# Three decoder mixers on one core: weight splits moved, transposes regrouped, buffers of matmul operands at other places

## What is computed

```
proj = rmsnorm(x) @ w_in                     # 512 x (512 + 512 + 64 + 2048)
c_q, c_kv, k_rope, gate = split(proj)
q  = rmsnorm(c_q) @ w_uq                     # per head 128 (nope) + 64 (rope)
kv = rmsnorm(c_kv) @ w_ukv                   # per head 128 (k) + 128 (v)
s  = (q_nope . k_nope + rope(q_rope) . rope(k_rope)) * scale, causal
y  = softmax(s) @ v
x  = x + (y * silu(gate)) @ w_out
```

## Time and profile before

| | |
|---|---|
| median of 3 runs | 2184.48 us (2184.06 to 2184.57) |
| the profiled execution | 2184.52 us |
| its span, first to last instruction | 2182.7 us |
| busy: PE, DVE, ACT, POOL | 99%, 66%, 45%, 6% of the span |
| matmuls | 10142 |
| DRAM traffic | 107 GB/s over the span |

### The profile page before, as it was taken

The page is one execution under the profiler, slowest core; times in us unless marked ns, Lnnn a source line. Parts: engine busy times, 40 slices in busy tenths (PEclk is TensorE's granted clock), DMA queues, the critical chain, the costliest instruction groups (busy, mean ns, idle before and its releaser), DMA issues. The chain is left out here.

```text
span 2182.7 us, 31173 instructions
## 1 busy us (share of the span) xinstructions
PE 2155.4 (99%) x10142; PEld 1791.6 (82%) x10142; DVE 1450.5 (66%) x2648; ACT 978.8 (45%) x1910; POOL 137.1 (6%) x161
## 2 busy tenths in 40 slices
PE   8999999999999999999999999999999999998999
PEld 6878888888888888888888888888888888887787
DVE  6677777777832568888888833676767676767432
ACT  5444444444432435555555633445453545355221
POOL 0100000000211000000000122200000000002000
PEclk9999999999999999999999999999999999999999
DMA  7312222222734623333333553532333233324542
GB/s 222 95 54 82 82 82 82 82 82 74 241 85 113 186 78 86 86 87 87 86 86 84 185 146 88 176 95 78 108 89 108 77 108 89 105 80 149 186 132 67
DMA packets 371436, 235.03 MB, mean 108 GB/s; under 512 B 5056, under 2 KB 345280, under 8 KB 371392
## 3 DMA queue, kind: packets, MB, share of 16 engines
q1 hardware_dynamic: 369264, 230.27, 36.8%
q10 hardware_dynamic: 2128, 4.19, 0.5%
HBM read 210.33 MB, written 24.12 MB: 107 GB/s over the span
## 5 line engine op out<-in xcount | busy, mean ns | idle before, releaser
L595 PE MATMUL pp<-act_hi,w_hi 128*128 128x512 f32 x2304 | 911.6, 396 | 11.7 <-DVE w_lo L569 9.2
L597 PE MATMUL pp<-act_hi,w_lo 128*128 128x512 f32 x2304 | 901.4, 391 | 0.0
L596 PE MATMUL pp<-act_lo,w_hi 128*128 128x512 f32 x2304 | 900.3, 391 | 0.0
L569 DVE TENSOR_TENSOR w_lo<-raw,w_hi 128x512 fp32r<-128x512 f32 x676 | 457.5, 703 | 308.4 <-ACT w_hi L560 305.1
L560 ACT ACTIVATE w_hi<-raw 128x512 fp32r<-128x512 f32 (+1 forms) x692 | 403.7, 620 | 336.7 <-PE pp L597 150.4
L595 PEld LDWEIGHTS pp<-act_hi,w_hi 128*128 128x128 f32 x2304 | 434.3, 188 | 98.8 <-DVE w_lo L569 9.4
L597 PEld LDWEIGHTS pp<-act_hi,w_lo 128*128 128x128 f32 x2304 | 433.7, 188 | 92.8
L596 PEld LDWEIGHTS pp<-act_lo,w_hi 128*128 128x128 f32 x2304 | 434.3, 189 | 84.9 <-issue 0.2
L1763 ACT ACTIVATE s_prob<-ps,s_minus 128x256 f32<-128x256 f32 x128 | 59.4, 469 | 84.4 <-DVE s_minus L1841 79.0
L1140 ACT ACTIVATE prob<-ps,minus,q_scale 128x512 f32<-128x512 f32 (+1 forms) x64 | 39.0, 615 | 100.6 <-DVE minus L1202 100.6
L595 PE MATMUL pp<-c_hi,w_hi 128*128 128x512 f32 x192 | 77.3, 403 | 3.3 <-DVE square L1240 1.4
(11 more groups left out here) (369 smaller groups left out, 2639.7 us busy)
## 6 DMA issues: line engine op xcount, KB each, us to landing
raw<-w_in SPq DMA_DIRECT2D x48, 1024.0 KB, 5.8
raw<-swa_w_in SPq DMA_DIRECT2D x36, 1024.0 KB, 5.6
raw<-mla_w_in SPq DMA_DIRECT2D x23, 1024.0 KB, 5.9
raw<-mla_w_out SPq DMA_DIRECT2D x16, 1024.0 KB, 6.8
raw<-swa_w_out SPq DMA_DIRECT2D x16, 1024.0 KB, 6.4
raw<-w_out SPq DMA_DIRECT2D x16, 1024.0 KB, 6.9
raw<-mla_w_ukv SPq DMA_DIRECT2D x16, 512.0 KB, 4.4
x_feature_major<-xT SPq DMA_DIRECT2D x8, 1024.0 KB, 8.7
```

The costliest lines, as they stand in the source:

```text
L569: q.eng.tensor_tensor(dst, raw_piece(tile, p), high, ALU.subtract).then_inc(s_lo, 1)
L595: q.eng.matmul(psum[:, :], wh, ah, start=start and n == 0, stop=False)
L596: q.eng.matmul(psum[:, :], wh, al, start=False, stop=False)
L597: last = q.eng.matmul(psum[:, :], wl, ah, start=False, stop=stop and n == PIECE // P - 1)
```

## The change

**Splits.** Up's four pieces of head 0 are split during the end of "in": three behind the last c tile, the fourth behind kt_hi and kt_lo. Body 0 of "mla" no longer splits them. rq moves ahead of kr_lo on DVE. ACT gets a one-element Tanh behind kr_hi; it writes to inv, which nothing has used yet.

**Turned blocks.** In "mla" vt stands behind gate piece 1, directly ahead of t3; t0 stands directly behind t1, goes to the third quarter of pt1 and waits for norm0 alone. pt_hi1 now waits for t0, pt_hi0 follows it, and pt_lo1 waits for pt_hi0; both steps of block 0 stand ahead of the tanh, the gate's eviction and q_sum. In "stick" t0, pt_hi0 and pt_lo0 stand directly behind those of block 1.

**Places.** A 128-byte buffer "gap" stands behind root, so that all that follows begins 128 bytes later; s_sink, 16 bytes in a slot of 32, moves behind s_q_scale, and d_w_hi, d_w_lo, d_ones, d_xc_hi and d_xc_lo stand further ahead. First bytes in a partition, as the buffers' sizes give them:

| buffer | before | mod 256 | after | mod 256 |
|---|---|---|---|---|
| act_lo, act_hi | 16512, 49280 | 128 | same | 128 |
| w_hi, w_lo | 98432, 114816 | 128 | same | 128 |
| acc (vT) | 135936 | 0 | same | 0 |
| c_hi, c_lo | 144128, 160512 | 0 | 144256, 160640 | 128 |
| kn_hi, qn_hi, kr_hi, pT_hi, v_hi | 199936, 189696, 185088, 213248, 204032 | 0 | + 128 | 128 |
| pairk_hi, pair | 182016, 175872 | 0 | + 128 | 128 |
| s_q_a, s_q_b, s_prob, s_pT_hi, s_pT_lo | 188448, 190496, 192544, 200736, 204832 | 32 | + 96 | 128 |
| d_q_hi, d_k_hi, d_pT_hi, d_v_hi | 147200, 153344, 178944, 159488 | 0 | + 128 | 128 |
| d_xc_hi, d_w_hi, d_ones | 196384, 219936, 222240 | 32 | 194944, 192384, 194432 | 128 |

Chunks and blocks within them are multiples of 512 bytes apart, so they share their buffer's last column.

The diff, without the lists in STEPS, which follow the order above:

```
@@ -367,6 +367,7 @@
         root = sb("root", [P, S])
+        sb("gap", [P, 32])
 
@@ -415,14 +416,14 @@
             pairk_hi, pairk_lo = sb("pairk_hi", [P, S], F32R, scope), sb("pairk_lo", [P, S], F32R, scope)
-            s_sinks, s_sink = sb("s_sinks", [P, 2, H2], F32, scope), sb("s_sink", [P, 2, 2], F32, scope)
+            s_sinks = sb("s_sinks", [P, 2, H2], F32, scope)
             s_q, s_q_a, s_q_b = sb("s_q", [P, S], F32, scope), sb("s_q_a", [P, S], F32R, scope), sb("s_q_b", [P, S], F32R, scope)
...
                 "s_minus", "s_total", "s_sinkexp", "s_inv"))
-            s_q_scale = sb("s_q_scale", [P, NB], F32, scope)
+            s_q_scale, s_sink = sb("s_q_scale", [P, NB], F32, scope), sb("s_sink", [P, 2, 2], F32, scope)
             s_cos, s_sin = sb("s_cos", [P, S], F32, scope), sb("s_sin", [P, S], F32, scope)
@@ -436,20 +437,20 @@
             d_pT_hi, d_pT_lo = sb("d_pT_hi", [P, PT_STEP * 3 + S], F32R, scope), sb("d_pT_lo", [P, PT_STEP * 3 + S], F32R, scope)
+            d_w_hi, d_w_lo = sb("d_w_hi", [P, 2, P], F32R, scope), sb("d_w_lo", [P, 2, P], F32R, scope)
+            d_ones = sb("d_ones", [P, P], F32R, scope)
             with ExitStack() as late:
                 y_lru = sb("y_lru", [P, H3 - 1, S], F32, late)
+            d_xc_hi, d_xc_lo = sb("d_xc_hi", [P, S], F32R, scope), sb("d_xc_lo", [P, S], F32R, scope)
             d_x, d_xc = sb("d_x", [P, S + CONV - 1], F32, scope), sb("d_xc", [P, S], F32, scope)
-            d_xc_hi, d_xc_lo = sb("d_xc_hi", [P, S], F32R, scope), sb("d_xc_lo", [P, S], F32R, scope)
             d_r, d_i, d_a = (sb(n, [P, S], F32, scope) for n in ("d_r", "d_i", "d_a"))
...
             d_w = sb("d_w", [P, 2, P], F32, scope)
-            d_w_hi, d_w_lo = sb("d_w_hi", [P, 2, P], F32R, scope), sb("d_w_lo", [P, 2, P], F32R, scope)
             d_rate, d_half_a, d_half_x, d_t, d_u, d_z, d_z2 = (
...
             d_gq = sb("d_gq", [P, 1], F32, scope)
-            d_ones = sb("d_ones", [P, P], F32R, scope)
             d_gate, d_th, d_sq = square[:, 0, :], root, square[:, 1, :]
@@ -957,12 +958,17 @@
                     q.eng.activation(rope_sin[0:ROPE1, :], rope_table[ROPE1:P, :], ACT.Copy).then_inc(*q.did("rope_sin"))
-            q.eng.activation(fold_hi[:, :], c("fold"), ACT.Copy)
+                if k == KROPE - 1:
+                    for p in range(3):
+                        hi(q, Tile("mla", 0, 1), p)
+                    q.eng.activation(fold_hi[:, :], c("fold"), ACT.Copy)
             copy_hi(q, qr_hi[:, :], qr[:, :], "kt_hi")
+            hi(q, Tile("mla", 0, 1), 3)
             rms_A(q, ps[2], R1, "T.norms", "root_q", root_q)
...
             copy_hi(q, kr_hi[:, :], pt[1][:, :], "kr_hi")
+            q.eng.activation(inv[:, 0:1], c("one", 0), ACT.Tanh)
 
@@ -994,12 +1000,16 @@
                     q.eng.tensor_tensor(scaled_table, rope_table[:, :], rstd[:, :], ALU.mult).then_inc(*q.did("scaled"))
+                if k == KROPE - 1:
+                    for p in range(3):
+                        lo(q, Tile("mla", 0, 1), p)
             q.eng.wait_ge(*q.at("A.kt_hi"))
             sub_lo(q, qn_lo[:, :], qr[:, :], qr_hi[:, :], "kt_lo")
+            lo(q, Tile("mla", 0, 1), 3)
+            q.eng.wait_ge(*q.at("A.root_q"))
+            q.eng.reciprocal(rstd_q, root_q).then_inc(*q.did("rq"))
             q.eng.wait_ge(*q.at("A.kr_hi"))
             sub_lo(q, kr_lo[:, :], pt[1][:, :], kr_hi[:, :], "kr_lo")
-            q.eng.wait_ge(*q.at("A.root_q"))
-            q.eng.reciprocal(rstd_q, root_q).then_inc(*q.did("rq"))
             q.eng.wait_ge(*q.at("A.root_kv"))
@@ -1023,7 +1033,7 @@
         SCORE = [ps[0][:, 0:256], ps[0][:, 256:512], ps[1][:, 0:384], ps[2][:, 0:512]]
-        PT_BANK = [pt[0], pt[1], pt[0], pt[1]]
+        PT_BANK = [pt[1][:, 2 * P:], pt[1], pt[0], pt[1]]
         def query_block(pT, b):
@@ -1056,11 +1066,11 @@
             if attn:
+                gate_piece(1)
                 q.eng.wait_ge(*q.at("V.v", i - 1))
...
                 m.then_inc(*q.did("vt"))
-                gate_piece(1)
             if not proj:
@@ -1080,6 +1090,7 @@
             turn(1, "V.pt_lo3")
+            turn(0, None)
             if not proj:
@@ -1089,7 +1100,6 @@
                 multiply_stacked(q, up, pp[1])
-            turn(0, "V.pt_lo2")
             if proj:
@@ -1121,7 +1131,7 @@
             def up_hi(p):
-                if proj:
+                if proj and attn:
                     hi(q, up, p)
@@ -1150,7 +1160,7 @@
                 if attn:
-                    q.eng.wait_ge(*q.at(f"T.t{b}"))
+                    q.eng.wait_ge(*q.at(f"T.t{b if b > 1 else 0}"))
                     copy_hi(q, query_block(pT_hi, b),
@@ -1159,6 +1169,7 @@
             turned_hi(1)
+            turned_hi(0)
             next_hi(1)
@@ -1167,7 +1178,6 @@
                 q.eng.activation(q_cos, pp[1][ROPE1:P, :], ACT.Copy).then_inc(*q.did("q_low"))
-            turned_hi(0)
             next_hi(3)
@@ -1225,13 +1235,14 @@
                 if attn:
-                    q.eng.wait_ge(*q.at(f"A.pt_hi{b}"))
+                    q.eng.wait_ge(*q.at(f"A.pt_hi{b if b > 1 else 0}"))
                     sub_lo(q, query_block(pT_lo, b), PT_BANK[b][:, 0:(b + 1) * P].rearrange("p (j n) -> p j n", n=P),
...
             turned_lo(1)
+            turned_lo(0)
             if not proj:
@@ -1242,7 +1253,6 @@
                 q.eng.tensor_tensor(q_sum, pp[1][0:ROPE1, :], q_cos, ALU.add).then_inc(*q.did("q_sum"))
-            turned_lo(0)
             if proj:
@@ -2272,7 +2282,7 @@
                 if attn:
-                    q.eng.wait_ge(*q.at("A.pt_hi3_e" if b == 3 and not proj else f"A.pt_hi{b}"))
+                    q.eng.wait_ge(*q.at("A.pt_hi3_e" if b == 3 and not proj else f"A.pt_hi{b if b > 1 else 0}"))
                     sub_lo(q, query_block(d_pT_lo, b), PT_BANK[b][:, 0:(b + 1) * P].rearrange("p (j n) -> p j n", n=P),
```

More of the change, by code:

```diff
@@ L98 @@
         "V": ("rstd ev0 lo0 ev1 lo1 a00 a01 a02 a03 a04 a05 a06 a07 r0 ev2 lo2 ev3 lo3 scaled ev4 lo4 ev5 lo5 ev6 "
-              "lo6 ev7 lo7 ev8 kt_lo kr_lo rq rkv scale z1 z2").split(),
+              "lo6 ev7 lo7 ev8 kt_lo rq kr_lo rkv scale z1 z2").split(),
         "G": "sum0 sum1 sum2 sum3 sum4 sum5 sum6 sum7".split(),
@@ L103 @@
         "T": "s3 s2 s1 s0 vt t3 t2 t1 t0 pv".split(),
-        "A": "exp3 exp2 exp1 exp0 v_hi pt_hi3 pt_hi2 pt_hi1 tanh q_low pt_hi0 qn_hi qr_hi kn_hi".split(),
+        "A": "exp3 exp2 exp1 exp0 v_hi pt_hi3 pt_hi2 pt_hi1 pt_hi0 tanh q_low qn_hi qr_hi kn_hi".split(),
         "V": ("mask3 top3 minus3 mask2 top2 mask1 top1 mask0 top0 minus inv3 norm3 inv0 norm2 norm1 norm0 v_lo "
-              "pt_lo3 pt_lo2 pt_lo1 gate q_sum pt_lo0 q_sin0 q_sin1 q_cos qr qn_lo qr_lo kn_ev kn_lo y silu v").split(),
+              "pt_lo3 pt_lo2 pt_lo1 pt_lo0 gate q_sum q_sin0 q_sin1 q_cos qr qn_lo qr_lo kn_ev kn_lo y silu v").split(),
     },
```

34 lines of the change are left out of this document (18 added, 16 removed).

## The result

| | before | after |
|---|---|---|
| median | 2184.48 us (2183.99 to 2186.15, 5 runs) | 2173.14 us (2171.64 to 2174.41, 5 runs) |
| ratio to before | | 0.9947, 95% interval 0.9937 to 0.9958 |
| span of the profiled execution | 2182.7 us | 2171.3 us |

The account below looks back on a forecast made before the run. PE, busy 99% of 2182.7 us, was taken as the bound throughout. 2184.5 - 4.2 (splits) - 1.1 (turned blocks) - 13.6 (places) = 2165.6 us, range 2162 to 2170, given 72%.

Parts of the forecast that it names:

- Part 1: Head 0 of "mla": splitting its weights earlier lets the scores start near 134.6, 4.2 us earlier, bounds 3.5 to 4.9.
- One cover: Head 0's fold: k_rope's eviction slips 0.9 us, qn_lo ends at 113.3, hidden by the norms product with 0.8 us to spare.
- Part 2: Turned blocks side by side in "mla" and "stick": fewer edges of transpose runs, 1.1 us, bounds 0 and 1.6.
- The merge of the values' run: "mla" heads: values' transposes join block 3's, saving 0.027 us behind the run and some 0.01 at its entry, 16 times: 0.6.
- there is nothing to win in 'mla': Block 0's single transpose in "mla" costs 0.11 us net, as it would in a run, so moving it gains nothing.
- Part 3: Buffers that stream or load as weights, apart from acc, placed 128 past a multiple of 256: 13.6 us, bounds 0 and 15.2.
- "swa", "stick" and the act pieces behind slow groups: Faster matmuls at the new places: 3.4 us in "swa", 1.4 in "stick", 1.5 for act matmuls behind slow groups.
- if the place sets the pace: Each moved matmul of c, scores, PV, "swa" and "stick" falls to 0.2266 us per 512 columns, 0.443 ns per column.
- A: Buffer places do nothing, the pace comes from what surrounds c: 2179.2 us, 11%.
- B: Only part of the slow pace is cured, half of the gain from buffer places: 2172.4 us, 8%.
- C: Block 1's turn waits for pt_lo3 in each head, 0.2 us x 16, 3.2 us: 2168.8 us, 6%.
- D: Streams and weights share one residue and their reads collide in all 2000 matmuls, 6.6 ns each: slower, 2192.4 us, 3%.

Follow-up runs that it names:

- The probe: Changed kernel plus 50 runs of 15 matmuls at chosen stream and weight places, at the start of head 0 of "mla"; 2308.25 us, only spacings read.
- two halves: Changed kernel with some 512-column act matmuls of output products 1 and 2 issued as two of 256 columns; 2177.33 us, 0.9965.

## Why the prediction was right and wrong

**Part 1, 4.2 us: right.** Against the norms product, from which the chain was counted, the scores of head 0 start 21.87 us later and not 26.07:

```profile
112.81 1.02 PE L922 MATMUL ps<-acc,con 128*128 128x512 f32 x2
```

is the norms product's start in before, and 113.01 in after; that is 4.20 us. The 0.2 by which this execution was late were lost ahead of it. The remaining wait is 0.56 (I said 0.5), for qn_lo, and splits alone gave 4.1 by the medians. One cover was thinner than I said: the three subtractions didn't go where DVE had been idle, they ran until 112.11, when the eviction started, and qn_lo of the fold ended at 114.17 where I had 113.3. PE took up the fold at 114.32: 0.15 us to spare, not 0.8. I had taken the idle time ahead of the eviction as if the pieces were ready then; ACT made their high parts only from 109.19.

**Part 2, 1.1 us: too low, 2.0 to 2.4.** The merge of the values' run gave 39 ns per body, as worked out (37). The term that was too small is block 0's, "there is nothing to win in 'mla'". The transpose itself costs the same in the run, but QN and gate piece 2 together get 33 ns shorter with turned blocks alone, gate piece 3 13, KN 17 and V 23. The likely reason is that a switch of kind throws the matmuls behind it off their pace, and without block 0's turn there is one less; I had that effect in hand, at the earlier trace rows, and applied it once. No run moves block 0 alone, and why V gains, which stands behind PV, isn't shown.

**Part 3, 13.6 us: the mis-sized term.** The places are worth 4.4 us. By terms, per body of "mla" with places alone:
- c, forecast 0.28: 0.20 (QR, QN, KN and V with block 0's turn take 10362 ns before and 10161).
- Scores, forecast 0.10: 0.007. PV, 0.06: 0.004. The act pieces, 0.03: -0.035, a loss.
- "swa", "stick" and the act pieces behind slow groups, 6.3 us in all: 2.25 with places alone ("kv" 0.22, "swa" 0.92, up to "stick" 0.08, "stick" 1.03). Of the 1.03 in "stick" 0.8 is in act pieces and 0.2 in d_xc and d_q, which are 512 wide; scores and PV there hold 0.06. In "swa" PV gets 59 ns per pair shorter and the scores 18 ns longer.

The step that failed is "if the place sets the pace, each of these matmuls falls to 0.2266 per 512 columns, 0.443 ns per column". It fails twice. It carried the pace of 512 columns over to 384 and 256, of which the earlier trace rows shows none; the only rows with narrow matmuls, were all slow, and I read that as the fault of their place without a fast narrow one to compare. The probe has 120.0 ns for 256 columns at equal residues, the slowest of its pairs, and not 113.4. And it took each buffer's own place for the cause, where it is the distance. By the table of places kn and qn, pT and v, d_k and d_q, d_pT and d_v lay on a multiple of 256 together before and lie at 128 together now, so for scores and PV of "mla" and "stick" the distance didn't change at all. With c alone moved, and kn and qn still at 0, the five scores of 512 columns take 227 to 231 ns each, nearly as in after (226 to 227): what was slow in them before came with the slow c matmuls ahead of them. The sum stays all the same, since the narrower ones get slower in turn (those of 384 columns 174.4 ns before, 176.9 with c alone). For "swa" the prediction misread the table, too: only the scores' weights and PV's stream lay 32 past, pairk and pair on a multiple of 256. The inference that was called one, that c falls wholly to 0.2266 at its new place, was right, though for another reason than the place by itself.

**The rivals.** A (places do nothing) falls with c alone and with w alone at 0. B was near in time (2172.4) and wrong in cause: c is cured whole, and the 6.8 us that B left to the places are still 2.4 too many, which the surplus of part 2 (1.3) partly hid. C did not come: no wait at block 1's turn. D (same residue collides) is the reverse of what happens at 512 columns, but it is what happens at 256, 120.0 on the diagonal.

The rules of the Trainium skill that rival A rested on ("SBUF — State Buffer", sections "Who interferes with whom" and "Operand start alignment"; "TensorE: Matmul & The Clock Gate", section "Back-to-back issue gap") have no term for where stream and weights lie (the line N/2.4 + 2.5 ns is given there for an isolated matmul). The pace of equal shapes moved by 3% and the kernel by 39 us with one gap of 128 bytes, so by measurement there is one.

## What to carry to other kernels

Read the pace from the starts, never from a busy share; compare equal shapes, and where they differ, look at the addresses of the stream and of the weights relative to each other (here: equal mod 256 for 512 columns). Carry a measured pace over to another shape only with a row of that shape. A change of kind in PE's stream (a transpose, a narrow product) cost time behind it here (27 ns behind two halves, 39 per body for the turn of the values that was merged), so side by side is better than spread out; and a probe of chosen shapes and places, put into a quiet stretch of the kernel, gave in one run the map that the whole kernels could only hint at.
